# Attention heads in another order: the next head's later sums ahead of this head's values, scores three heads ahead, partial row sums on GpSimd

## The reference

```python
def sb_weights(z, valid):
    log_stay = jnp.where(valid, jax.nn.log_sigmoid(-z), 0.0)
    log_after = lax.cumsum(log_stay, axis=z.ndim - 1, reverse=True) - log_stay
    return jnp.where(valid, jnp.exp(jax.nn.log_sigmoid(z) + log_after), 0.0)

def sb_attend(qb, qpos, k, v, kpos, bias):
    z = sb_logits(qb, k, bias)          # q.k * scale + bias
    a = sb_weights(z, kpos[None, :] < qpos[:, None])
    return jnp.einsum('bhqk,bkhd->bqhd', a.astype(v.dtype), v)
```

## Time and profile before

| | us |
|---|---|
| median of 3 runs | 1549.87 (1549.57 to 1550.96) |
| the profiled execution | 1550.86 |
| its span, first to last instruction | 1548.9 |
| TensorE busy | 1413.1 (91%) |
| VectorE busy | 787.1 (51%) |
| ScalarE busy | 509.5 (33%) |
| GpSimd busy | 147.0 (9%) |

### The profile page before, as it was taken

The page is one execution under the profiler, slowest core; times in us unless marked ns, Lnnn a source line. Parts: engine busy times, 40 slices in busy tenths (PEclk is TensorE's granted clock), DMA queues, the critical chain, the costliest instruction groups (busy, mean ns, idle before and its releaser), DMA issues.

```text
span 1548.9 us, 28016 instructions
## 1 busy us (share of the span) xinstructions
PE 1413.1 (91%) x10682; PEld 1290.0 (83%) x10682; DVE 787.1 (51%) x2988; ACT 509.5 (33%) x776; POOL 147.0 (9%) x228
## 2 busy tenths in 40 slices
PE   5979978879999787879997999998989999999998
PEld 3979965568988787769776788898989999999998
DVE  4578747657889878752344421344243333232222
ACT  3323345526844322220223432223232222222212
POOL 1000012122320533100320000000000000000000
PEclk9999999989999878976989999998999999999999
DMA  9359944534532423429989999923223333333222
GB/s 324 97 190 294 296 171 165 163 124 135 172 101 70 123 61 103 122 65 279 313 306 314 362 344 311 308 76 117 82 59 92 96 96 91 88 92 89 76 76 79
DMA packets 254473, 252.56 MB, mean 163 GB/s; under 512 B 22433, under 2 KB 215083, under 8 KB 254309
## 3 DMA queue, kind: packets, MB, share of 16 engines
q1 hardware_dynamic: 254341, 250.79, 50.8%
HBM read 235.66 MB, written 15.29 MB: 162 GB/s over the span
## 4 chain that ended last, share of the span: by engine, by line
PE 76%; DVE 9%; DMA 4%; ACT 4%; POOL 3%; issue 2%; SPq 1%; POOLq 0%; ACTq 0%; DVEq 0%
PE ps L1044 54%; PE ps L1073 3%; PE ps L1141 3%; PE ps L1152 2%; DMA wring<-in_w_ffn_out 2%; PE ps L1425 2%; PE ps L1444 1%; DVE wring L2096 1%; DVE kring L2096 1%; PE ps L1342 1%; PE ps L1085 1%; DVE R L2161 1%; DMA out_rec_sample<-R 1%; POOL R L2802 1%; POOL R L2648 1%
## 5 line engine op out<-in xcount | busy, mean ns | idle before, releaser
L1044 PE MATMUL ps<-obT_split,wring_split 128*128 128x268 f32 (+2 forms) x1296 | 265.2, 286 | 0.0
L1044 PE MATMUL ps<-obT_split,qv_split 128*128 128x260 f32 (+2 forms) x1040 | 219.1, 292 | 12.7 <-DVE wring_split L587 11.2
L587 DVE TENSOR_TENSOR wring_split<-wring,vring_split 128x1024 fp32r<-128x1024 f32 (+1 forms) x92 | 110.5, 1201 | 236.0 <-ACT vring_split L581 236.0
L1044 PEld LDWEIGHTS ps<-obT_split,wring_split 128*128 128x128 f32 (+1 forms) x1296 | 202.0, 189 | 0.7
L1044 PE MATMUL ps<-obT_split,vring_split 128*128 128x260 f32 (+1 forms) x960 | 197.6, 287 | 0.8 <-issue 0.8
L1044 PE MATMUL ps<-xn_split,vring_split 128*128 128x260 f32 (+1 forms) x960 | 194.6, 284 | 4.1 <-DVE obT_split L601 4.1
L1044 PEld LDWEIGHTS ps<-obT_split,qv_split 128*128 128x128 f32 (+1 forms) x1040 | 162.1, 190 | 37.0 <-issue 34.4
L1044 PE MATMUL ps<-xn_split,qv_split 128*128 128x260 f32 (+2 forms) x912 | 187.0, 287 | 0.0
L1614 ACT ACTIVATE R<-ps 128x520 f32<-128x520 f32 (+1 forms) x86 | 52.5, 611 | 372.5 <-PE ps L1044 372.5
L587 DVE TENSOR_TENSOR wring_split<-wring,qv_split 128x1024 fp32r<-128x1024 f32 (+1 forms) x73 | 91.7, 1256 | 146.4 <-ACT qv_split L581 146.3
L1044 PEld LDWEIGHTS ps<-xn_split,vring_split 128*128 128x128 f32 x960 | 149.0, 190 | 4.9 <-issue 4.2
(11 more groups left out here) (391 smaller groups left out, 2191.4 us busy)
## 6 DMA issues: line engine op xcount, KB each, us to landing
wring<-in_w_in SPq DMA_DIRECT2D x72, 512.0 KB, 5.7
kring<-in_cache_k SPq DMA_DIRECT2D x64, 512.0 KB, 5.0
vring<-in_cache_v SPq DMA_DIRECT2D x64, 512.0 KB, 6.2
kring<-in_cache_v SPq DMA_DIRECT2D x64, 512.0 KB, 5.6
wring<-in_w_ffn_in SPq DMA_DIRECT2D x44, 512.0 KB, 3.8
vring<-in_cache_k SPq DMA_DIRECT2D x24, 512.0 KB, 4.8
R<-in_cache_k SPq DMA_DIRECT2D x24, 512.0 KB, 7.0
wring<-in_cache_k SPq DMA_DIRECT2D x16, 512.0 KB, 3.7
```

The costliest lines, as they stand in the source:

```text
L587: nc.vector.tensor_tensor(fr(w_part(wlo[:, p % RING, :], p)), w_part(wring[:, p % RING, :], p), w_part(w_high(p), p), ALU.subtract).then_i ...
L1044: last = mm(ps[0:m, 2 * (t % 2) + i, 0:n], fr(w), fr(x[k][:, a + i * n:a + i * n + n]), start=(k == 0 and w is w_h and x is hi), stop=(k = ...
```

## The change

TensorE runs later_sums(h+1), values(h), scores(h+3); before the loop stand later_sums(0) and scores(2). ScalarE runs weights(h+1), copy(h), scaled(h+3), softplus(h+3). VectorE runs the subtractions of h, softplus(h+1), then the pages. GpSimd runs the z mask of h, a new `tail_sums(h+1)`, and the softplus mask of h+2. `tail_sums` adds rows of the masked softplus: for block k of 1 to 3, `tails[k]` is the sum of blocks k to 4 over the columns that lie past block k's own 128 queries: 272 columns for k = 1, 144 for k = 2 and 16 for k = 3. It has five adds, of which two wait for earlier ones. later_sums(h) then has for each block a triangle product, one ones product with the next block over 128 columns, and one with `tails` for the rest: 12 products in place of 15. `s_msp` now counts four steps a head.

```diff
--- before.py
+++ after.py
@@ -377,6 +377,7 @@
               qv[:, 2:4, :].rearrange("p a n -> p (a n)")[:, 0:SB_ALL]]
         sps = at(SBT + SB_ALL, 2, SB_ALL)
         es = at(21056 - SB_ALL, SB_ALL)
+        tails = {k: at(SBT + 3 * SB_ALL + o, LP - P * (k + 1)) for k, o in ((1, 0), (2, 272), (3, 416))}
 
         cT = at(0, NQKV, TOKENS)
         oaT = at(0, H, TOKENS)
@@ -1128,18 +1129,22 @@
                     m.then_inc(s_s, 1)
 
                 def later_sums(h):
-                    pe.wait_ge(s_msp, h + 1)
+                    pe.wait_ge(s_msp, 4 * h + 4)
                     if h == 0:
                         pe.wait_ge(tok_a, 2 * H)
                     else:
                         pe.wait_ge(s_arg, h)
                     for kt, a, b, bank, col in SB_PIECES:
-                        parts = [(tri_ge, kt, a)] + [(ones, k2, max(a, P * k2)) for k2 in range(kt + 1, TT)
-                                                     if P * k2 < b]
-                        for j, (lhs, k2, q) in enumerate(parts):
-                            f = sb_at(k2, q)[2]
-                            m = mm(ps[:, 3 + bank, col + q - a:col + b - a], lhs[:, :],
-                                   sps[:, h % 2, f:f + b - q], start=(j == 0), stop=(j == len(parts) - 1))
+                        f, near, far = sb_at(kt, a)[2], P * (kt + 1), P * (kt + 2)
+                        parts = [(tri_ge, a, b, sps[:, h % 2, f:f + b - a])]
+                        if near < b:
+                            e, f = min(far, b), sb_at(kt + 1, near)[2]
+                            parts.append((ones, near, e, sps[:, h % 2, f:f + e - near]))
+                        if far < b:
+                            parts.append((ones, far, b, tails[kt + 1]))
+                        for j, (lhs, q, e, rhs) in enumerate(parts):
+                            m = mm(ps[:, 3 + bank, col + q - a:col + e - a], lhs[:, :], rhs,
+                                   start=(j == 0), stop=(j == len(parts) - 1))
                     m.then_inc(s_c, 1)
 
                 def values(h):
@@ -1157,11 +1162,14 @@
                 scores(1)
                 head_tokens(vbT, 1, 6)
                 head_tokens(vbT, 1, 7)
+                later_sums(0)
+                scores(2)
                 for h in range(H):
-                    later_sums(h)
-                    if h + 2 < H:
-                        scores(h + 2)
+                    if h + 1 < H:
+                        later_sums(h + 1)
                     values(h)
+                    if h + 3 < H:
+                        scores(h + 3)
 
                 pe.wait_ge(s_z, H + 2)
                 pe.wait_ge(s_arg, H)
@@ -1679,20 +1687,27 @@
                     act.wait_ge(s_exp, h + 1)
                     go(es, es, ACT.Ln, bias=1.0).then_inc(s_ln, 1)
 
+                def weights(h):
+                    act.wait_ge(s_marg, h + 1)
+                    go(zs[h % 3], zs[h % 3], ACT.Exp).then_inc(s_w, 1)
+
                 head_tokens(vtok, 1, 5)
                 softplus(0)
                 head_tokens(vtok, 1, 6)
                 scaled(1)
                 head_tokens(vtok, 1, 7)
                 softplus(1)
+                scaled(2)
+                weights(0)
+                softplus(2)
                 for h in range(H):
-                    act.wait_ge(s_marg, h + 1)
-                    go(zs[h % 3], zs[h % 3], ACT.Exp).then_inc(s_w, 1)
-                    if h + 2 < H:
-                        scaled(h + 2)
-                        softplus(h + 2)
+                    if h + 1 < H:
+                        weights(h + 1)
                     act.wait_ge(s_av, h + 1)
                     nc.scalar.copy(qbT[:, h, META:LP], ps[:, 6, :]).then_inc(s_o, 1)
+                    if h + 3 < H:
+                        scaled(h + 3)
+                        softplus(h + 3)
 
             def silu_conv(n):
                 act.wait_ge(cv_step, (CW - 1) * (n + 1))
@@ -2151,8 +2166,7 @@
                     v.scalar_tensor_tensor(sps[:, h % 2, :], zs[h % 3], 0.0, es, ALU.max, ALU.add)\
                         .then_inc(s_sp, 1)
 
-                for h in (0, 1):
-                    softplus(h)
+                softplus(0)
                 for h in range(H):
                     dve.wait_ge(s_c, h + 1)
                     for b in range(3):
@@ -2161,10 +2175,10 @@
                         m = v.tensor_tensor(zb, zb, ps[:, 3 + b, 0:w], ALU.subtract)
                     m.then_inc(s_arg, 1)
 
+                    if h + 1 < H:
+                        softplus(h + 1)
                     for b, p in K_PAGES["att", 2 * h] + K_PAGES["att", 2 * h + 1]:
                         k_page(b, p)
-                    if h + 2 < H:
-                        softplus(h + 2)
 
             def conv(n):
 
@@ -2684,6 +2698,23 @@
                     m = keep(buf[:, f:f + n], buf[:, f:f + n], [[1, n]], a - P * kt, -1, ALU.is_gt, fill)
                 m.then_inc(sig, 1)
 
+            def tail_sums(h):
+
+                pool.wait_ge(s_msp, 4 * h + 1)
+                if h:
+                    pool.wait_ge(s_c, h)
+
+                def row(k, a, b):
+                    f = sb_at(k, a)[2]
+                    return sps[:, h % 2, f:f + b - a]
+                g_.tensor_tensor(tails[3], row(3, 4 * P, LP), row(4, 4 * P, LP), ALU.add).then_inc(s_msp, 1)
+                g_.tensor_tensor(tails[1][:, 0:P], row(1, 2 * P, 3 * P), row(2, 2 * P, 3 * P), ALU.add)
+                g_.tensor_tensor(tails[2][:, 0:P], row(2, 3 * P, 4 * P), row(3, 3 * P, 4 * P), ALU.add)
+                pool.wait_ge(s_msp, 4 * h + 2)
+                g_.tensor_tensor(tails[2][:, P:P + 16], row(2, 4 * P, LP), tails[3], ALU.add).then_inc(s_msp, 1)
+                pool.wait_ge(s_msp, 4 * h + 3)
+                g_.tensor_tensor(tails[1][:, P:P + 144], row(1, 3 * P, LP), tails[2], ALU.add).then_inc(s_msp, 1)
+
             pool.wait_ge(ab_d, AB_G)
             g_.tensor_copy(gP[:, 0:32], gt[:, 0:32]).then_inc(ab_p, 1)
             keep(gP[:, 32:40], gt[:, 32:40], [[0, H]], LASTP - 1, -1).then_inc(ab_p, 1)
@@ -2693,6 +2724,8 @@
                 if h >= 0:
                     pool.wait_ge(s_arg, h + 1)
                     causal(zs[h % 3], NEG, s_marg)
+                if 0 <= h + 1 < H:
+                    tail_sums(h + 1)
                 if h + 2 < H:
                     pool.wait_ge(s_sp, h + 3)
                     causal(sps[:, h % 2, :], 0.0, s_msp)
```

## The result

The changed kernel took 1560.91 us (median of five runs, 1556.97 to 1563.96), the kernel before beside it 1549.87: a ratio of 1.0064, 95% interval 1.0044 to 1.0083. Its profiled execution was the fastest of the five, 1556.97 us with a span of 1555.3, 6.4 above the span of before. The same kernel, run again later beside other kernels, came out at 1557.08 (ratio 1.0033, 1.0020 to 1.0047). So it is slower, as forecast, by 6.6 to 11 us as a median where 5.1 was forecast. The first median, 1560.91, lies above the forecast's own range (1551.5 to 1559) and at the very edge of the whole one (1544.5 to 1561); the second lies inside both.

What follows compares the result with a forecast made beforehand. Bound: an attention ring of 13.36 us a head, TensorE idling until exp is done. Terms -2.0 + 8.3 + 2.0 - 1.6 - 1.6 = +5.1 us: 1555.0 median, 1556.0 profiled; own range 1551.5 to 1559, whole 1544.5 to 1561.

Steps and rivals of the forecast that it cites:

- The ring: Attention heads: serial turn of sums, subtractions, softplus, ten selects, five adds; 8.42 us outside the sums, 13.08 in all.
- steps 1 and 2: TensorE's new order closes through GpSimd's queue; subtractions with start 1.71 us, softplus 1.57, both groups of selects 3.10.
- The adds: GpSimd's five tail adds a head, on the new ring: 2.0 us taken, between 1.19 and 2.8.
- Rival A: GpSimd's adds pipeline like selects, tails 1.4 us, fewer clock falls: -5.9 us, 1544; chance 0.18.
- rival B: GpSimd's adds are blocked by VectorE's page products, tails 2.8 us: +6.4 us, 1561; chance 0.12.
- Shorter sums: TensorE's later sums stream fewer columns of ones: 1.13 us saved a head, from 5.79 to 4.66.
- step 7: TensorE's gaps before sums lower its clock: five short ones at 1.56 us, two long at 2.4; +8.3 us net.
- Rival C: Low clock mostly falls on values and scores, which have 2.9 us of cover: +0.4 us, 1550.3; chance 0.19.
- The start: First later sums of the attention stage: +2.0 us waiting for tails, -1.6 as they take 6.6 us.
- step 8: Ends of the attention stage: first sums +2.0 and -1.6 us; last values, behind a 1.9 us gap, -1.6.
- the chain carries the shift on: After the attention stage, TensorE's weight tiles start 0.8 us later, as before, and the stage's shift persists to the end.
- Rival D: Attention ring not closed through GpSimd's queue; a turn is VectorE's 11 us: -16 us, 1534; chance 0.03.

Runs made afterwards that it cites:

- Experiments 1 and 3: experiment 1, and the changed kernel without the adds (15 products as before, new order kept): 1536.73 us, ratio 0.9913.
- experiment 1: Changed kernel with VectorE making softplus two heads ahead again, as in the kernel before: 1538.26 us, ratio 0.9929.
- experiment 2: Changed kernel with unread 512-column products put into TensorE's list ahead of each head's later sums: 1544.36 us, ratio 0.9958.
- experiment 8: Changed kernel run once more, unaltered, for a second profile: 1557.08 us (1553.83 to 1561.64).
- the control: Kernel before with only unread products added ahead of the values (2, and 4 for the last two heads): 1548.21 us, ratio 0.9983.
- experiment 4: Kernel before with tail_sums and the 12 products, every order as before: 1551.08 us, ratio 1.0004.

## Why the prediction was right, and where it wasn't

- *The ring* (steps 1 and 2). As forecast: subtractions, softplus, ten selects, adds, sums. Outside the sums 8.30 us against 8.42. Experiments 1 and 3 took pieces of it out and the turn fell to 12.3 and 11.9.
- *The adds*: 261.12 to 263.24, 2.12 us, against 2.0. Rival A (under 1.6) and rival B (2.8) fall both, though B's time, 1561, is the one nearest to the first median. The 0.3 us for two waits in B's bound came from no row; the trace has 0.07 us of idle ahead of the last add.
- *Shorter sums*: 5.69 us to 4.30, 1.39 saved, against 1.13. Products of ones saved 1.23 of it, against 1.13 by columns; the other 0.16 is in triangle products that are the same in both kernels, and why those got shorter isn't shown.
- *The clock* (step 7). The term decided the sign. Warm turns of 12.60 against 13.36 would have gained. The seven sums took 6.3, 5.8, 7.3, 6.0, 6.0, 5.7 and 7.2 us, 14.2 more than 7 x 4.30; 12.6 were forecast. The two behind long gaps cost 4.9 (4.8 forecast), the five behind short ones 9.3 (7.8 forecast, from the price of values). Rival C (most of it covered) fell; experiment 2 shows it by taking it away.
- *The start*: the first sums wait 1.9 us longer behind softplus (219.15 - 214.34 against 218.28 - 215.34), against 2.0. They took 7.15 us (to 226.30, where scores start), before 8.02 by the same measure: -0.9 against -1.6.
- *The end* (step 8) failed. "A gap of 1.9 us, so they run at 2.82" was 2.69 us and 4.49. The copy of head 6 stands behind exp of head 7 in ScalarE's list, and the last values wait for it, as L1707 in their bracket says; I had let the values wait for exp alone. From the end of the last sums to the end of the stage it was 10.0 us against 9.3 before, by the same measure: +0.7 in place of -1.6.
- *Summed*: +1.9 start, -0.9 first sums, +4.5 turns (226.30 to 328.64 is 102.3, against 97.8), +0.7 end = +6.2 for the stage, which began 1.0 us earlier and ended 5.2 later (338.62 against 333.41). That it began earlier is not explained. Two misses nearly cancel: the turns cost 4.5 where 6.3 were forecast, since sums saved more, and the end cost 2.3 more than forecast. That the profiled execution, 1556.97, came within 1 us of the 1556.0 forecast for it is in part luck.
- *Behind the stage* "the chain carries the shift on" held only roughly: +5.3, +5.7, +7.3, +6.2, +6.4 us at five places in one profile and +5.6, +6.1, +8.2, +9.0, +9.6 in the other. The rest of the 11 us of the first median must come from there, since the stage repeats; no profile of an execution at that median was taken, and apart from the 1.9 us named in experiment 8 its cause stays open.

Rival D, that the change does what its words say, fell. With the adds left out the time (1536.73) comes near D's 1534, but the mechanism is still not D's: the ring closes through GpSimd's queue all the same, in 11.88 us.

## What to carry to other kernels

Follow the new order through each queue before counting overlap: a step moved off one engine's path can put three of another's on it. Price the gap ahead of each burst of matmuls at both clock levels, and ask whether the burst behind it is on the ring; here 14 us hung on that, and a few unread products bought most of them back. The gap's length alone doesn't tell whether the clock falls (experiment 1), and a gain in one stage can be lost to the clock in a later one (the control), so look at both. When a VectorE instruction with two SBUF inputs is long, don't count GpSimd selects beside it.

## What the hardware showed that was not expected

The same gap of 2.21 us was followed by the low clock in one of six turns of the kernel before (turns of 13.36 us) and in all six of experiment 4's (turns of 13.66, 258.60 to 272.26): a repeated turn can meet it each time. In experiment 1 gaps of 2.55 and 3.52 us were not followed by it, one of 2.54 was. A GpSimd select of 112 columns took 1.46 us beside a VectorE instruction of 1.55 us with two SBUF inputs, and 0.33 to 0.41 beside products of 0.28 to 0.36.
